# Output product of a hybrid layer: plain products for each tile, against seven half-size products for each pair of tiles with two of the operand sums on GpSimd

## The chip, the core and the metric

The kernel runs on one core of one Trainium2 chip. The time is that of the device in microseconds (us), from one launch; less is better. Everything is computed in float32.

## The reference

A model layer is applied to a prompt of 4096 rows of 1024 values and to a sample stream of 64 rows with an earlier state. The rows are normalised and modulated (h), multiplied with `w_in` (1024 x 3328) and split into a retention part (four heads with a state of 128 x 128 each) and a windowed attention part (eight query heads, two key heads, a sink in each softmax). Both give 512 columns a row, and these are multiplied with `w_out`:

```python
r_out = _head_norm(r_out).reshape(B, L, RET_WIDTH).astype(x.dtype) * jax.nn.silu(rg)
...
a_out = a_out * jax.nn.silu(ag)
y = jnp.concatenate([r_out, a_out], axis=-1) @ w_out
x = x + gate * y
...
y_prompt = _rmsnorm(xp, final_g)
```

The product with `w_out` (1024 x 1024) over all rows is what the change rewrites.

## The kernel before

The rows are cut into 33 tiles of 128: 32 of the prompt (`NT`), and one (`SAMPLE`) whose lower half is the sample. TensorE gets float32 accuracy from three passes: each operand is split into a rounded high part and the remainder (`hh`/`hl`, `wh`/`wl`), and `dense` adds high x high, high x low and low x high in one PSUM bank. A product of a tile with 512 columns of weights is thus 3 x 8 matmuls of 128x512; two such products make a tile's output, 48 matmuls.

There are two phases, each a loop over the tiles (`phase_tiles`), and each engine has its own program; semaphores order them. Phase A (`slot`) makes the four 512-column groups of the retention half, the retention itself, and writes each tile's h and its gated retention rows `yr` to DRAM scratch. Phase B (`slot_b`) loads h again, makes keys and values (`dense_kv`, 24 matmuls of 128x256), queries and gates (two products), the scores of the tile before (`scores`), masks them and takes the row maximum (`mask_max` on VectorE), takes the exponentials (`softmax` on ScalarE), turns p by a round trip through DRAM and a block transpose (`turn_p`), weighs the values (`weigh`), and makes the output of the tile two back from `yr` and the attention rows, with its gate, the residual, the final norm and the store.

The order within a tile is that of the code on each engine. All transfers are issued by SyncE's queue (SP) in program order; one that waits holds back all behind it. `store_blocks` and `load_blocks` issue four transfers each.

## Time and profile before

| | |
|---|---|
| median of 3 runs | 1877.16 us (1875.1 to 1878.53) |
| the profiled execution | 1879.75 us, span of its core 1878.0 us |
| TensorE busy | 1811.4 us, 96% of the span |
| VectorE busy | 1158.3 us, 62% |
| ScalarE busy | 533.6 us, 28% |
| GpSimd busy | 114.3 us, 6% |
| DMA | 314.23 MB, 60.0% of the 16 engines |
| TensorE in the chain that ended last | 90% of the span |

Busy shares are averages over the phases. The chain of waits follows the last instruction back to what released each step, so it tells which engine the time went through.

### The profile page before, as it was taken

What the parts mean: (1) busy time and instruction counts of PE and PEld (TensorE: products, weight loads), DVE (VectorE), ACT (ScalarE), POOL (GpSimd) and SP (SyncE); (2) the same over time, 40 slices, a digit from 0 to 9 for tenths busy, and PEclk for the clock granted to TensorE, in tenths of its full rate; (3) what the DMA queues carried; (4) which work ended last, traced back from release to release, by engine and by line L of the source; (5) the groups of instructions that cost most, each with busy time, mean ns of one, the idle gap of its engine ahead of it and who ended that gap; (6) DMA issues with size and microseconds to landing.
All of it is one profiled execution on the core that took longest, in us unless ns stands there. A gap on an engine that the chain in (4) does not pass through costs nothing.

```text
span 1878.0 us, 30820 instructions
## 1 busy us (share of the span) xinstructions
PE 1811.4 (96%) x9636; PEld 1499.0 (80%) x9636; DVE 1158.3 (62%) x2742; ACT 533.6 (28%) x1471; POOL 114.3 (6%) x278
## 2 busy tenths in 40 slices
PE   6899999999999999999699999999999999999995
PEld 3678888888888888888578888888888888888884
DVE  3655666556566655667566676666666666666664
ACT  3312212212221221223332333333333333333321
POOL 1000000000000000010000000000000000000000
PEclk8999999999999999999899999999999999999998
DMA  9655555555555555554667567557567567566573
GB/s 373 226 153 141 128 149 144 128 140 139 136 134 148 145 125 144 136 152 131 186 176 211 158 172 210 158 174 206 162 177 198 166 181 192 167 186 190 160 187 102
DMA packets 489513, 314.23 MB, mean 167 GB/s; under 512 B 349554, under 2 KB 424498, under 8 KB 488452
## 3 DMA queue, kind: packets, MB, share of 16 engines
q1 hardware_dynamic: 489476, 313.77, 60.0%
q8 instruction: 19, 0.31, 0.1%
q14 instruction: 18, 0.15, 0.0%
HBM read 183.31 MB, written 130.36 MB: 167 GB/s over the span
## 4 chain that ended last, share of the span: by engine, by line
PE 90%; issue 4%; DMA 3%; DVE 1%; SPq 1%; POOL 0%; ACT 0%; POOLq 0%; DVEq 0%; ACTq 0%
PE bank L1245 78%; PE bank L1439 3%; PE bank L1418 3%; PE bank L1343 1%; PE bank L1335 1%; PE bank L1341 1%; PE bank L1329 1%; DMA xn_scratch<-xn 1%; DMA aqk_row<-aqk_scratch 1%; SPq L402 1%; PE bank L1398 0%; DMA xp<-xn_scratch 0%; SPq L489 0%; DMA out_gate<-gate_scratch 0%; POOL small L621 0%
## 5 line engine op out<-in xcount | busy, mean ns | idle before, releaser
L1245 PE MATMUL bank<-wh,hh 128*128 128x512 f32 x1584 | 400.9, 395 | 15.3 <-DVE k_row L904 6.1
L1245 PE MATMUL bank<-wl,hh 128*128 128x512 f32 x1584 | 393.2, 391 | 0.0
L1245 PE MATMUL bank<-wh,hl 128*128 128x512 f32 x1584 | 393.1, 390 | 0.0
L1245 PEld LDWEIGHTS bank<-wh,hh 128*128 128x128 f32 x1584 | 294.4, 190 | 77.3 <-issue 12.3
L1245 PEld LDWEIGHTS bank<-wl,hh 128*128 128x128 f32 x1584 | 298.6, 189 | 62.3
L1245 PEld LDWEIGHTS bank<-wh,hl 128*128 128x128 f32 x1584 | 298.3, 188 | 62.0
L703 ACT ACTIVATE hf<-xn,tiny_a 128x128 f32<-128x128 f32 (+1 forms) x248 | 98.6, 480 | 374.0 <-DVE xn L879 374.0
L1172 DVE SCALAR_TENSOR_TENSOR a_gate<-a_gate,bank 128x128 f32<-128x128 f32 x132 | 29.1, 283 | 205.8 <-ACT a_gate L836 205.8
L775 ACT ACTIVATE s_row<-p_in,tiny_b 128x256 f32<-128x256 f32 x264 | 130.9, 500 | 49.8 <-DVE tiny_b L1082 49.8
L1245 PE MATMUL bank<-wh,yh 128*128 128x512 f32 x528 | 133.1, 395 | 6.9 <-DVE yl L1113 6.9
L1245 PE MATMUL bank<-wl,yh 128*128 128x512 f32 x528 | 130.4, 389 | 0.0
L1245 PE MATMUL bank<-wh,yl 128*128 128x512 f32 x528 | 130.4, 389 | 0.0
L1245 PEld LDWEIGHTS bank<-wh,yh 128*128 128x128 f32 x528 | 100.8, 191 | 28.3 <-DVE yl L1113 7.1
L1245 PEld LDWEIGHTS bank<-wl,yh 128*128 128x128 f32 x528 | 99.1, 188 | 20.6
L1245 PEld LDWEIGHTS bank<-wh,yl 128*128 128x128 f32 x528 | 99.1, 188 | 20.6
L1007 DVE SCALAR_TENSOR_TENSOR r_gate<-r_gate,bank 128x512 f32<-128x512 f32 x33 | 22.7, 688 | 140.1 <-ACT r_gate L751 140.1
L1076 DVE CUSTOM_DVE_ANT_0 p_in<-bank,mask 128x256 f32<-128x256 f32 x264 | 96.2, 421 | 1.1 <-issue 1.1
L1090 DVE STREAM_TRANSPOSE s_row<-p_in 128x1024 f32<-128x1024 f32 x66 | 81.6, 1237 | 3.4 <-DMA p_in<-p_scratch 3.3
L924 DVE TENSOR_TENSOR s_t<-bank,decay 128x512 f32<-128x512 f32 x33 | 22.8, 692 | 94.9 <-PE bank L1329 94.9
L836 ACT ACTIVATE a_gate<-bank 128x256 f32<-128x256 f32 x66 | 21.7, 381 | 156.8 <-PE bank L1245 156.8
L664 POOL TENSOR_TENSOR v_prev<-v_row,small 128x128 f32<-128x128 f32 x31 | 12.4, 399 | 858.4 <-PE bank L1439 858.4
L879 DVE STREAM_TRANSPOSE xn<-xp 128x1024 f32<-128x1024 f32 x31 | 38.6, 1245 | 41.2 <-DMA xp<-xn_scratch 41.2
(159 smaller groups left out, 2289.9 us busy)
## 6 DMA issues: line engine op xcount, KB each, us to landing
p_scratch<-s_row SPq DMA_DIRECT2D x264, 128.0 KB, 2.2
p_in<-p_scratch SPq DMA_DIRECT2D x66, 512.0 KB, 4.4
xt<-in_x_prompt SPq DMA_DIRECT2D x64, 512.0 KB, 3.8
h_scratch<-hf SPq DMA_DIRECT2D x33, 512.0 KB, 2.9
hf<-h_scratch SPq DMA_DIRECT2D x33, 512.0 KB, 4.7
out<-xt SPq DMA_DIRECT2D x32, 512.0 KB, 4.9
xn_scratch<-xn SPq DMA_DIRECT2D x31, 512.0 KB, 2.9
xp<-xn_scratch SPq DMA_DIRECT2D x124, 128.0 KB, 3.1
```

Of the source, the lines that this page charges most:

```text
L703: last = nc.scalar.activation(hf[:, k, lo:P], src, ACT.Identity, bias=h_shift[:, k, c:c + 1], scale=h_scale[:, k, c:c + 1])
L775: nc.scalar.activation(s_row[:, half].rearrange("p b (j s c) -> p b j s c", j=4, s=2)[:, :, j, :, :], p_in[:, half, j, :].rearrange("p (s ...
L836: last = nc.scalar.activation(blocked(a_gates[u][:, cols]), by_blocks(ag_bank(i, t)[:, cols]), ACT.Tanh, scale=0.5)
L879: V.transpose(xn[:, :], xp[:, :]).then_inc(x_turned, 1)
L924: V.tensor_tensor(s_t[:, :], qs_b[:, :], decay[:, :], ALU.mult).then_inc(st_done, 1)
L1007: V.scalar_tensor_tensor(r_gate[:, :], r_gate[:, :], 1.0, za1[:, :], ALU.add, ALU.mult).then_inc(rg_done, 1)
L1076: last = V.tensor_tensor_reduce(out=p_in[:, half, j, :], in0=src, in1=m, scale=1.0, scalar=MASKED, op0=ALU.add, op1=ALU.max, accum_out=s_m ...
L1090: V.transpose(s_row[:, half].rearrange("p b n -> p (b n)"), p_in[:, half].rearrange("p b n -> p (b n)")).then_inc(pt_done, 1)
L1172: last = V.scalar_tensor_tensor(ag, ag, 1.0, z, ALU.add, ALU.mult)
L1245: ins = mm(out, a[:, k, :], b[:, k, :], start=first and n == part[0] and k == chunks[0], stop=last and n == part[-1] and k == chunks[-1])
L1418: last = mm(s_banks[2 * half + g][:, jl * 2 * P:(jl + 1) * 2 * P], q[rows, 2 * half + jl, :], k[rows, :, :], start=n == 0, stop=n == 2, ti ...
L1439: last = mm(qv_b[cols, half * 2 * P:(half + 1) * 2 * P], v, p_t[:, :, :, g, s, :], start=s == 0, stop=s == 1, tile_position=(0, g * HD))
```

## The change

The output product leaves phase B and becomes a third phase, C, over pairs of tiles (`phase_pairs`, `window`). Of a pair, the two tiles' `yr` halves are a11 and a21, their attention halves a12 and a22. From these, four sums are made (S1 = a21 + a22, S2 = S1 - a11, S3 = a11 - a21, S4 = a12 - S2), each of 128x512, and seven products of 12 matmuls of 128x512 (`product`, in the order 1, 6, 5, 7, 2, 4, 3) with seven blocks of `w_out`, three of which are themselves sums; seven additions combine the products to the pair's four output quarters. The sample's half pair uses four plain products. S1 and S3 of most pairs are made by GpSimd (`raw_pool`), S2 and S4 by VectorE (`raw_sum`). Here GpSimd also adds the residual (`add_x`), ScalarE makes the high parts (`high`) and VectorE the low ones (`low`).

Around it: the weight blocks are made in phase A's tiles 5 to 12 (`load_prep`, `store_prep`, sums and splits on VectorE and ScalarE), written to scratch, and loaded by GpSimd's queue in phase B (six of 1 MB in its tiles 2 to 7, two in the tiles 30 and 31, six behind the last input product). `yr` is turned in phase A, five tiles late, instead of in phase B. Phase B writes its attention rows to scratch. It turns p two tiles back, its scores stay in PSUM (`mask_max` writes in place, `softmax` reads there), and the high part of h is made by VectorE. The four 1 MB pieces of the gate weights are loaded one a tile (tiles 0 to 3) and used in tile 4, and not all in tile 0.

```diff
+                if static(i) and t < 4:
+                    load_piece(sp, FIRST_GATE + t)
...
-                if mid:
-                    for half in range(2):
-                        wait(sp, exp_done, 2 * (t - 1) + half + 1)
-                        store_blocks(p_dram[2 * (t - 1) + half], s_row[:, half], p_stored[half])
-                    p_back(*prev, 0)
+                if back:
+                    p_back(*same, 0)
+                    gate_out(*same)
+                    p_back(*same, 1)
...
-                    p_back(*prev, 1)
-                    wait(sp, gate_scaled, t)
-                    store_blocks(g_dram[t - 1], a_gates[1 - u][:, :].rearrange("p (b n) -> p b n", b=4), g_stored)
+                    p_out(*prev, 0)
...
+                    p_out(*prev, 1)
...
+            def add_x(i, u, n):
+                p = 2 * i + u
+                xq = xqs[u]
+                src, at = ((c22f, D + COLS), (c11f, 0), (u3f, D), (u2f, COLS))[n]
+                wait(pool, gated, 4 * p + n + 1)
+                wait(pool, xq_loaded[u], 32 * i + 32)
+                nc.gpsimd.tensor_tensor(xq[:, at:at + COLS], xq[:, at:at + COLS], src, ALU.add).then_inc(added, 1)
...
+            def raw_pool(i, u, n):
+                p = 2 * i + u
+                held = {7: 3, 5: 5}[n]
+                wait(pool, op_hi[held], p)
+                wait(pool, op_lo[held], p)
+                wait(pool, in_loaded[u], 64 * i + 64)
+                if n == 5:
+                    wait(pool, raw_done[6], p)
+                    nc.gpsimd.tensor_tensor(s1f, operand_in(u, 0), operand_in(u, 4), ALU.add).then_inc(raw_done[5], 1)
+                else:
+                    nc.gpsimd.tensor_tensor(s34f, operand_in(u, 1), operand_in(u, 0), ALU.subtract).then_inc(raw_done[7], 1)
...
-                    nc.scalar.activation(s_row[:, half].rearrange("p b (j s c) -> p b j s c", j=4, s=2)[:, :, j, :, :],
-                                         p_in[:, half, j, :].rearrange("p (s b c) -> p b s c", s=2, b=4), ACT.Exp,
+                    src = s_banks[2 * half + j % 2][:, (j // 2) * 2 * P:(j // 2 + 1) * 2 * P]
...
-                    last = V.tensor_tensor_reduce(out=p_in[:, half, j, :], in0=src, in1=m, scale=1.0, scalar=MASKED,
+                    last = V.tensor_tensor_reduce(out=src, in0=src, in1=m, scale=1.0, scalar=MASKED,
...
+                if not static(i) or t >= 3:
+                    gated_values(*older)
+                    scale_gate(*same)
+                if mid:
+                    turn_qk(*prev)
+                    qk_low(*prev)
+                if back:
+                    turn_p(*same, 0)
+                    turn_p(*same, 1)
...
+            def raw_sum(i, u, n):
...
+                elif n == 6:
+                    wait(dve, raw_done[5], p + 1)
+                    wait(dve, raw_done[3], p)
+                    V.tensor_tensor(s2f, s1f, a11, ALU.subtract).then_inc(raw_done[6], 1)
+                elif n == 3:
+                    wait(dve, raw_done[6], p + 1)
...
+            def low(i, u, n):
+                p = 2 * i + u
+                wait(dve, op_hi[n], p + 1)
+                raw = ops_raw[n] if n in ops_raw else operand_in(u, n)
+                V.tensor_tensor(ops[n][1], rows4(raw), ops[n][0].bitcast(F32), ALU.subtract).then_inc(op_lo[n], 1)
+            def sum_u2(i, u):
+                p = 2 * i + u
+                wait(dve, m1_kept, p + 1)
+                wait(dve, prod[6], p + 1)
+                wait(dve, added, 4 * p)
+                V.tensor_tensor(u2f, m1f, prod_bank[6][:, :], ALU.add).then_inc(summed, 1)
+            def gate_mult(ap, half, count):
+                wait(dve, summed, count)
+                V.tensor_tensor(ap, ap, out_gate[:, half * COLS:(half + 1) * COLS], ALU.mult).then_inc(gated, 1)
+            def out22(i, u):
+                p = 2 * i + u
+                wait(dve, prod[7], p + 1)
+                wait(dve, summed, 7 * p + 1)
+                wait(dve, added, 4 * (p - 1) + 3)
+                V.tensor_tensor(u3f, u2f, prod_bank[7][:, :], ALU.add).then_inc(summed, 1)
+                wait(dve, prod[5], p + 1)
+                wait(dve, summed, 7 * p + 2)
+                V.tensor_tensor(c22f, u3f, prod_bank[5][:, :], ALU.add).then_inc(summed, 1)
+                V.tensor_tensor(u2f, u2f, prod_bank[5][:, :], ALU.add).then_inc(summed, 1)
+                gate_mult(c22f, 1, 7 * p + 3)
+            def out11(i, u):
+                p = 2 * i + u
+                wait(dve, prod[2], p + 1)
+                wait(dve, added, 4 * (p - 1) + 2)
+                V.tensor_tensor(c11f, m1f, prod_bank[2][:, :], ALU.add).then_inc(summed, 1)
...
+            def final(i, u):
+                p = 2 * i + u
+                wait(dve, rms_step, 3 * p + 3)
+                for n in range(1 if static(i) and p == LAST else 2):
+                    x = xqs[u][:, n * D:(n + 1) * D]
+                    V.scalar_tensor_tensor(x, x, out_rstd[:, n:n + 1], fin_g[:, :], ALU.mult, ALU.mult).then_inc(fin_done, 1)
...
+            def window(i, u):
...
+                if not static(i) or p < LAST:
+                    low(i, u, 3)
+                if not static(i) or p <= LAST:
+                    out12(*before)
+                if not static(i) or p + 1 <= LAST:
+                    low(*nxt, 1)
+                if not static(i) or p < LAST:
+                    sum_u2(i, u)
+                if not static(i) or p + 1 < LAST:
+                    raw_sum(*nxt, 6)
+                final(*before)
+                if not static(i) or p + 1 < LAST:
+                    for n in (6, 5):
+                        low(*nxt, n)
+                if not static(i) or p < LAST:
+                    out22(i, u)
+                if not static(i) or p + 1 < LAST:
+                    low(*nxt, 7)
+                    raw_sum(*nxt, 3)
+                if not static(i) or p < LAST:
+                    out11(i, u)
+                if not static(i) or p + 1 <= LAST:
+                    low(*nxt, 2)
+                if not static(i) or p < LAST:
+                    out21(i, u)
+                if not static(i) or p + 1 < LAST:
+                    low(*nxt, 4)
+                if static(i) and p == LAST:
...
+                if front:
+                    dense_kv(i, u)
+                    wait(pe, aq_done, t)
+                    dense(aq_b[:, :], *h_of(i, t), group(0)).then_inc(zb_ready, 1)
                     scores(*prev)
...
+                    wait(pe, ag_done, t)
+                    dense(ag_b[:, :], *h_of(i, t), group(1)).then_inc(zb_ready, 1)
...
+                    weigh(*same)
...
+            def product(i, u, n, weights=None, first=True, last=True):
+                p = 2 * i + u
+                wait(pe, op_hi[n], p + 1)
...
+                elif n_w == 7:
+                    wait(pe, squared, 4 * p)
+                elif n_w == 1:
+                    wait(pe, m1_kept, p)
+                else:
+                    read = {6: 1, 5: 4, 2: 5, 4: 6, 3: 7}[n_w]
+                    wait(pe, summed, 7 * (p - 1) + read)
+                out = prod_bank[5 if static(i) and p == LAST and n_w == 3 else n_w][:, :]
+                b = block_of[n_w]
+                weight = [[w_block(b, low)[:, j, :] for j in range(4)] for low in range(2)]
+                return dense(out, *ops[n], weight, chunks=range(4), first=first, last=last)
...
+                    product(i, u, 1).then_inc(prod[1], 1)
+                    product(i, u, 1, weights=5, last=False)
...
+                    product(i, u, 5).then_inc(prod[5], 1)
+                    product(i, u, 7).then_inc(prod[7], 1)
+                    product(i, u, 2).then_inc(prod[2], 1)
+                    product(i, u, 4).then_inc(prod[4], 1)
+                    product(i, u, 3).then_inc(prod[3], 1)
```

How instructions stand now, at three places. First SP's queue in phase B's loop. Before, behind the stores of p of tile t-1 (`p_scratch` is the DRAM scratch of p, `aqk_scratch` that of queries and keys):

```order
L489 DMA p_scratch<-s_row 32x4x256
L234 ISA
L514 ISA
L514 DMA p_in<-p_scratch 128x1024
L489 ISA
L489 DMA aqk_scratch<-aqk_row 32x4x160
L489 ISA
```

The changed kernel at the head of a tile, from the last transfer of the gate's store on:

```order
L596 DMA g_scratch<-a_gate 32x4x128
L626 ISA
L626 DMA p_in<-p_scratch 128x1024
L283 ISA
L641 ISA
L641 DMA ya_scratch<-ya_f 128x512
L636 DMA a_gate<-g_scratch 128x512
L596 ISA
L596 DMA aqk_scratch<-aqk_row 32x4x160
```

The second half of p (of tile t-2 now) comes back behind the gate's store; all eight stores of p of tile t-1 stand at the end of the tile, behind the queries' and keys' store.

Second, TensorE. Before, the second of the output's two 512-column products in phase B's loop (`yh`, `yl` are its operands), and the first rows of `weigh`:

```order
L1245 MATMUL bank<-wh,yh 128x512 x8
L1245 MATMUL bank<-wl,yh 128x512 x8
L1245 MATMUL bank<-wh,yl 128x512 x8
L234 REGISTER_ALU
L234 ISA
L1439 MATMUL bank<-s_row,v_prev 64x256 x2
L1439 MATMUL bank<-s_row,v_row 64x256 x2
```

The changed kernel, products 1 and 6 of a pair, the first two of its seven, in phase C's loop (`op_a` and `op_s` are the split operands):

```order
L1728 MATMUL bank<-wh,op_a_h 128x512 x4
L1728 MATMUL bank<-wl,op_a_h 128x512 x4
L1728 MATMUL bank<-wh,op_a_l 128x512 x4
L283 ISA
L1728 MATMUL bank<-wh,op_s_h 128x512 x4
L1728 MATMUL bank<-wl,op_s_h 128x512 x4
L1728 MATMUL bank<-wh,op_s_l 128x512 x4
```

Forty-eight matmuls a tile, 96 a pair, have become 84 a pair, and phase B's loop keeps none of them.

Third, VectorE in phase C's loop, from the low part of S4 to the final norm (`u` and `c` are partial outputs, `m_row` the kept product 1, `xq` the residual rows):

```order
L1563 TENSOR_TENSOR op_s_l<-s_raw,op_s_h 128x512
L283 ISA x2
L1607 TENSOR_TENSOR u<-u,bank 128x512
L283 REGISTER_ALU
L1575 TENSOR_TENSOR u<-u,out_gate 128x512
L283 REGISTER_ALU
L1563 TENSOR_TENSOR op_a_l<-in,op_a_h 128x512
L283 REGISTER_ALU
L1570 TENSOR_TENSOR u<-m_row,bank 128x512
L1552 TENSOR_TENSOR s_raw<-s_raw,in 128x512
L283 ISA
L1615 SCALAR_TENSOR_TENSOR xq<-xq,tiny_c,fin_g 128x1024 x2
```

and GpSimd in the same window:

```order
L875 TENSOR_TENSOR xq<-xq,u 128x512
L283 ISA x2
L887 TENSOR_TENSOR s_raw<-in 128x512
L895 TENSOR_TENSOR tiny_c<-tiny_c 128x2
L283 ISA
L897 TENSOR_TENSOR tiny_c<-tiny_c,small 128x2
L283 REGISTER_ALU x2
L900 TENSOR_TENSOR tiny_c<-tiny_c,small 128x2
L889 TENSOR_TENSOR s_raw<-in 128x512
```

None of this stood in the kernel before. GpSimd's row of line 875 waits for VectorE's row of line 1575, VectorE's of line 1570 for GpSimd's of line 875, and VectorE's of line 1552 for GpSimd's of line 887.

## Rows read from the trace of the kernel before

**Rows 1.** Chain of waits, phase A and phase B: start, length, what (us).

```profile
392.10 21.77 PE bank L1245 x96
...
1263.63 24.85 PE bank L1245 x120
```

**Rows 2.** Windows, one tile of phase A and one of phase B.

```profile
415.00:440.35 25.35, 25.35 (x130) 21.60 (x130) 15.61 (x34) 5.42 (x12) 1.95 (x4) 1.00 0.54 140
1263.63:1291.98 28.35, 28.35 (x161) 23.37 (x161) 18.31 (x50) 9.74 (x32) 1.33 (x4) 1.00 0.63 180
```

**Rows 3.** Timeline of TensorE between the phases: start, length, instruction [idle before].

```profile
894.69 1.20 PE L1245 MATMUL bank<-wkvh,hh 128*128 128x256 f32 x8
...
910.47 1.19 PE L1245 MATMUL bank<-wkvh,yh 128*128 128x256 f32 x8 [1.76 <-DVE a_gate L1172]
...
927.73 0.58 PE L1418 MATMUL bank<-ak_h,aq_h 64*128 64x256 f32 x2 [14.15 <-DVE ak_l L1199]
...
946.66 2.08 PE L1245 MATMUL bank<-wkvh,hh 128*128 128x256 f32 x8 [3.92 <-DVE hl L894]
```

**Rows 4.** Timeline of TensorE at the end.

```profile
1837.49 3.56 PE L1245 MATMUL bank<-wh,yh 128*128 128x512 f32 x8 [6.93 <-DVE yl L1113]
```

**Rows 5.** Timeline of TensorE and VectorE in phase A's tiles 1 and 2.

```profile
85.88 3.54 PE L1245 MATMUL bank<-wh,hh 128*128 128x512 f32 x8 [4.10 <-DVE k_row L904]
122.27 2.56 PE L1245 MATMUL bank<-wh,hh 128*128 128x512 f32 x8 [1.95 <-DVE k_row L904]
81.41 1.25 DVE L879 STREAM_TRANSPOSE xn<-xp 128x1024 f32<-128x1024 f32 x1 [8.39 <-DMA xp<-xn_scratch]
```

**Rows 6.** Timeline of SP's issues in a tile of phase B.

```profile
1267.23 4.20 SPq L489 DMA_DIRECT2D p_scratch<-s_row  x8
1271.57 0.37 SPq L514 DMA_DIRECT2D p_in<-p_scratch  x1
...
1275.69 1.81 SPq L489 DMA_DIRECT2D g_scratch<-a_gate  x4
```

**Rows 7.** Tile p_in: from issue to landing of its loads.

```profile
DMA to landing us min/median/max: 3.6/4.4/5.5
```

**Rows 8.** Timeline of VectorE and ScalarE: one half of a tile's softmax, from its mask on.

```profile
1263.15 0.06 DVE L1072 MEMSET small<- 128x1 f32 x1 [0.40 <-PE bank L1418]
...
1264.89 0.51 ACT L775 ACTIVATE s_row<-p_in,tiny_b 128x256 f32<-128x256 f32 x1 [1.47 <-DVE tiny_b L1082]
...
1266.87 0.19 ACT L779 ACTIVATE tiny_b<-tiny_b 128x4 f32<-128x4 f32 x1
```

**Rows 9.** Page, part 5: VectorE's transpose of p.

```profile
L1090 DVE STREAM_TRANSPOSE s_row<-p_in 128x1024 f32<-128x1024 f32 x66 | 81.6, 1237 | 3.4 <-DMA p_in<-p_scratch 3.3
```

**Rows 10.** Timeline of VectorE in phase A: three operations of 128x512.

```profile
415.41 0.69 DVE L902 TENSOR_TENSOR bank<-bank,rope 128x512 f32<-128x512 f32 x1
416.01 0.68 DVE L904 TENSOR_TENSOR q_row<-bank,rope 128x512 f32<-128x512 f32 x1
416.80 0.69 DVE L907 TENSOR_TENSOR q_row<-q_row,bank 128x512 f32<-128x512 f32 x1
```

**Rows 11.** Groups by line: VectorE's final norm.

```profile
L1145 DVE SCALAR_TENSOR_TENSOR xt<-xt,small,fin_g 128x1024 f32<-128x1024 f32 x33 | 42.2, 1279 | 2.0 <-POOL small L658 2.0
```

**Rows 12.** Timeline of GpSimd in phase B.

```profile
1262.10 0.40 POOL L664 TENSOR_TENSOR v_prev<-v_row,small 128x128 f32<-128x128 f32 x1 [26.85 <-PE bank L1439]
1262.46 0.19 POOL L654 TENSOR_TENSOR small<-small 128x1 f32<-128x1 f32 x1
...
1263.00 0.55 POOL L658 TENSOR_TENSOR small<-small 128x1 f32<-128x1 f32 x1
```

**Rows 13.** Timeline of GpSimd and VectorE near the start.

```profile
34.95 1.46 POOL L618 TENSOR_TENSOR small<-small 128x1 f32<-128x1 f32 x1 [27.16 <-ACT xn L682]
36.48 2.49 POOL L621 TENSOR_TENSOR small<-small 128x1 f32<-128x1 f32 x1
...
34.07 4.49 DVE L319 TENSOR_TENSOR wl<-stage,wh 128x2048 fp32r<-128x2048 f32 x2
```

1133 lines of the change are left out of this document (725 added, 408 removed).

## Prediction

> **What bounds the kernel now.** I read the chain of waits first, then the stretches by window, then single engines. In [rows 1] the chain runs through TensorE in equal pieces: 96 matmuls of 128x512 in 21.77 us in phase A, so 0.2268 us each, and 120 in 24.85 us in phase B. The second window of [rows 2] is one tile of phase B: 28.35 us long and TensorE busy for all 28.35, at a granted clock of 1.00 (2.4 GHz), while VectorE works 18.31 us and ScalarE 9.74. TensorE sets the pace, and whatever leaves it counts in full, as long as nothing else takes its place.
>
> A tile of phase B splits so: the 120 matmuls are 96 wide ones (21.77) and keys and values (24.85 - 21.77 = 3.08); the scores and the weighing are the rest, 28.35 - 24.85 = 3.50. The output product is 48 wide matmuls, 10.89 us.
>
> From the first key matmul at 894.69 [rows 3] TensorE has 33 x (3.08 + 10.89 + 3.50) = 576.5 us without the output, and 33 x 10.89 = 359.2 us of output. That would end at 1830.4; the span ends at 1878.0. The 47.6 us between are lost around the phases' ends: [rows 3] shows idle times of 1.76, 14.15 and 3.92 us, and behind each the matmuls are slow (eight of 256 columns take 2.08 us at 946.66 and 1.20 at 894.69). With about 4 us for that slowness (my estimate from these rows) the start of phase B costs 23.7 us. The end has the other 23.9, with the 6.93 us of [rows 4] in it.
>
> **The product itself.** A pair needs 84 wide matmuls, 19.05 us, where it needed 96, 21.77. Sixteen pairs take 304.8 us and the sample's four products of 12 again 10.9: 315.7 instead of 359.2, which saves 43.5 us. With no loss anywhere TensorE would be done at 1786.9. The seven additions, the sums and the splits are new work of the others; that decides the rest.
>
> **Start of phase A.** VectorE waits 8.39 us for a transfer in tile 1, with 4 MB of gate weights just ahead in the queue, and TensorE then 4.10; two pieces of `w_in` do the same in tile 2, 1.95 [rows 5]. With the slow matmuls behind them (3.54 and 2.56 us for eight, 1.81 at full pace) that is 8 us, and the change spreads or moves these loads. Against it stand four chunks of weight preparation, each 1 MB in and 3.5 MB out in two tiles. Since 4 MB in a burst cost about 6 us and 2 MB about 2.7, I take 2 us a chunk, 8 in all: net 0, bounds -8 and +8. VectorE's sums and splits there and the turn of `yr` lie in its idle time: 15.61 of 25.35 us are busy [rows 2]. Without that cover each would cost its 0.7 to 2.3 us a tile.
>
> **Start of phase B.** Keys have a bank of their own now, so the 1.76 us go. The scores of tile 0 stand behind the queries of tile 1, 8.5 us of work, and SP no longer issues weights, gate, norm weights and `yr` around the load of the queries and keys. What remains is the small load of the sinks, for which VectorE now waits ahead of the turn. I take 5 us idle and 1.5 slow: 6.5 in place of 23.7 (bounds 1 and 15).
>
> **Phase B's pace.** TensorE needs 17.47 us a tile. VectorE loses two gate products, two additions, the norm, a turn and three splits (about 6.6 us) and gets a copy of h, 0.7: 18.3 becomes 12.4, which fits. In-place masking is free by [rows 10], where line 902 writes PSUM in 0.69 us and line 904 SBUF in 0.68. The loop that matters is that of p. From the mask's first row to the end of its half's exponentials pass 3.91 us (1263.15 to 1267.06, [rows 8]). Then SP works in order: four stores 2.1 (half of 4.20), the load of queries and keys 0.37, four stores 2.1, the load of h 0.37, the first half of p 0.37, the gate's stores 1.81 [rows 6], about 0.15 between groups: 11.8 us after the mask the second half's load is issued. It lands 4.4 us later [rows 7], its turn takes 1.24 [rows 9], and behind that turn stands the next tile's mask: 17.4 us around, just TensorE's 17.47. DMA traffic a tile falls only from 5.1 to 3.9 MB (estimate from the sizes of the transfers) in 17.5 instead of 28.35 us, so I expect it to land a little later than now: 17.7 us a tile, +0.2 x 31 = 6.5 us. At the 5.5 us seen as longest it would be 18.5, +32; at 3.6 it is 0.
>
> **Start of phase C.** VectorE has some 49 us of work listed for the last tiles and pairs 0 and 1 where TensorE has 40, and 6 MB of late weights come in beside it. Half of the weights can wait, since products 1, 6, 5, 7 use blocks loaded long before. I take 5 us, bounds 2 and 15. The end behind the last matmul (sum, gate, residual, squares, three GpSimd steps, norm, store) I take as 9 us.
>
> **Phase C's pace.** VectorE has 20 operations of 128x512 and two norms a pair. Operations follow each other every 0.60 to 0.61 us, or 0.79 where one waits for the one before [rows 10]; a norm is 1.28 [rows 11]. Sixteen at 0.61, four at 0.79 and 2.56 make 15.5 us. GpSimd's price for 128x512 no row shows. Its 128x128 takes 0.40 and its one column 0.19 [rows 12], so by the slope about 1.03; the bounds are 0.69, VectorE's own, and 1.6, four times 0.40. In the chain between them (gate, `add_x`, `sum_u2`, S1, S2, the squares' three steps of 1.09 [rows 12], norm) the norm can start 0.69 + 0.05 + 1.03 + 1.03 + 1.09 = 3.9 us after the gate starts, while VectorE has 2.44 us of work: 1.45 idle. Without more that is 16.9 us, under 19.05.
>
> But [rows 13] shows the two engines in each other's way. GpSimd's one-column step takes 1.46 us and its power 2.49, where [rows 12] has 0.19 and 0.55, and both end just as one of VectorE's two subtractions of 2.29 us each (34.07 to 38.56) is over. Those read two tiles in SBUF. Thirteen of VectorE's twenty operations in a window and both norms do too, and all six of GpSimd's. If one keeps out the other, `add_x` falls three times between two such operations, once partly covered by one that reads a bank, and S3 once ahead of the norm: about 3.5 x 1.03 = 3.6 us. The window is then 15.5 + 1.45 + 3.6 = 20.5 us, VectorE paces it, and 15 windows cost 22 us more than TensorE's 19.05. I choose this over 19.05, because the trace shows the exclusion in one direction at least. The Trainium skill, page "SBUF — State Buffer", section "Who interferes with whom", says the same of both: a VectorE instruction with two SBUF inputs contends with a GpSimd instruction that reads SBUF, and who starts first keeps the other out to its end. The trace agrees for GpSimd (1.46 us against 0.19); that VectorE is held too, no row shows.
>
> The page "GPSIMD Engine Reference", section "Elementwise — side-by-side cycle accounting", gives 4497 ns for 2048 columns; scaled to 512 that is an estimate of 1.1 to 1.3 us, and the window would be 21 to 22 us by it.
>
> **The sum.** 1786.9 + 0 + 6.5 + 6.5 + 5 + 9 + 22 = 1836 us as a span, against 1878.0. The median of the runs shown is 0.8 below that span, so 1835.
>
> **Rivals.** *No hold:* VectorE is not kept out, and phase C runs at 19.05: 1813. For it speaks that no VectorE row is seen longer; against it [rows 13].
>
> *GpSimd's two sums do not relieve VectorE:* they take two operations, 1.2 us, off it, and hold it as long. A GpSimd operation of 1.2 to 1.3 us, between the slope and its upper bound, makes the window 21.6 to 22: 1852 to 1859. At 1.6 us it is 23.7, +48: 1883, slower.
>
> *Slower through SP's queue:* a wait takes the place of TensorE's work in phase B. The second half of p is behind 13 other issues; what is late is `turn_p`, behind it in VectorE's order the mask, then the scores' banks, then TensorE. The sum has room for 1878 - 1836 = 42 us, 1.4 us in each of 31 tiles. So a round of 19.1 us decides, with landings of 5.8 us or issues of 0.65 where [rows 6] has 0.52. For it: the round is already 17.4, with denser traffic; against it: 5.5 was the longest landing of 66. With six weight loads of 1 MB in tiles 2 to 7 it can hold there for some tiles. At 19.6 us it gives 1894.
>
> *Gains at the seams fail:* preparation and the two starts at their upper bounds, +25: 1860.
>
> **Chances and range.** The window at 19.5 to 21.5 us and the round near 17.7: 0.48, for 1820 to 1852. No hold: 0.20, for 1803 to 1820. A heavier hold, a round of 18 to 19, or the seams: 0.19, for 1852 to 1873. Within 0.2% (about what a measurement of this kernel can tell from no change, 3.8 us): 0.03. Slower, by the queue or the 23.7 us window: 0.10. Faster is 0.87. The range 1806 to 1870 takes in most of the first three.
>
> **What the changed profile would show.** Pairs of 84 matmuls in phase C with TensorE busy under 95%, at a distance of 20.5 us from pair to pair, VectorE over 85% busy in that stretch, and its subtractions or GpSimd's additions with single durations 0.5 to 1 us over their shortest. At 19.05 us and TensorE busy throughout, the hold was wrong. In phase B tiles 17.5 to 17.9 us apart; if more, VectorE waits at `turn_p` for p_in. The first scores come at about 923 us. GpSimd's 128x512 is at 1.0 to 1.3 us. I am wrong if phase B's tiles are over 18.5 us apart, or the windows over 22.

## The result and the profile after

The changed kernel takes 1974.01 us (median of 4 runs, 1967.41 to 1975.05), the kernel before 1876.22 (1875.1 to 1878.53): a ratio of 1.0516, 95% interval 1.0501 to 1.0531. It is 5.2% slower, where 1835 us was forecast and 1870 was the upper end. The profiled execution took 1975.05 us with a span of 1973.2.

The matmuls did become fewer. TensorE is busy 1806.8 us of that span, where it was 1811.4 of 1878.0, and that includes the matmuls at the lower clock behind each wait. What grew is its idle time: 1973.2 - 1806.8 = 166 us instead of 67. The other part of the loss is in the busy time itself. With 43.5 us of matmuls taken out it should be 1767.9, and it is 39 us more. Some 7 of these are TensorE's own tile of phase B, 17.69 us at a granted clock of 1.00 where the prediction has 17.47; most of the rest should be the lower mean clock, 0.972 instead of 0.985; it was not split further. The windows of the changed kernel say where (stretch, its length, busy time and instructions of each engine, granted clock, DMA share, GB/s); [rows 2] are their counterpart.

```profile
core 0: us, PE busy (x) PEld busy (x) DVE busy (x) ACT busy (x) POOL busy (x), PEclk, DMA share, GB/s
300.00:400.00 100.00, 87.93 (x413) 72.92 (x412) 67.06 (x127) 24.41 (x48) 5.86 (x12) 0.93 0.73 200
...
600.00:928.37 328.37, 326.91 (x1662) 278.00 (x1661) 218.45 (x442) 75.20 (x151) 24.79 (x49) 1.00 0.62 156
928.37:995.21 66.84, 49.88 (x284) 41.14 (x282) 28.11 (x95) 13.82 (x57) 5.40 (x10) 0.90 0.55 157
995.21:1098.85 103.64, 94.21 (x561) 76.49 (x561) 67.96 (x208) 32.55 (x133) 4.28 (x7) 0.93 0.83 252
1098.85:1476.99 378.14, 355.17 (x2243) 285.35 (x2241) 262.73 (x821) 127.31 (x517) 11.10 (x21) 1.00 0.72 214
...
1557.95:1614.34 56.39, 35.72 (x185) 28.20 (x185) 31.59 (x92) 17.41 (x61) 3.57 (x7) 0.82 0.97 330
...
1656.00:1950.00 294.00, 269.50 (x1137) 217.90 (x1136) 248.29 (x298) 98.17 (x214) 143.49 (x123) 0.97 0.39 141
```

From 600 us on, phase A runs as before: 326.91 of 328.37 us busy. Ahead of that, while the weights are prepared, TensorE loses an eighth (87.93 of 100, DMA share 0.73). The first keys stand at 928.37, where [rows 3] have 894.69. The start of phase B (928 to 995) loses 17 us, phase B itself 6 to 10% in every stretch, and the passage to phase C is the worst: 35.72 of 56.39 us busy, the 16 DMA engines 97% occupied at 330 GB/s. In phase C TensorE is busy 269.50 of 294 us, and VectorE 248.29.

| stretch of the profiled execution | forecast | measured | difference |
|---|---|---|---|
| first key matmul (all of phase A) | 894.7 | 928.4 | +33.7 |
| start of phase B, loss: 66.8 us to the fourth tile's keys, less 47.1 of work (keys and queries of three tiles 41.9, one and a half times 3.50) | 6.5 | 19.7 | +13.2 |
| 29 tiles of phase B | 17.7 each | 19.4 each (562.7) | +49.4 |
| passage to phase C, loss: 92.2 us from 1557.95 to pair 2's first product, less 60.9 of work | 5 | 31.3 | +26.3 |
| 14 windows of phase C | 20.5 each | 21.65 each (303.1) | +16.1 |
| end behind the last matmul | 9 | 9 | 0 |

The differences add up to 138.7 us; the span is 137.2 over the 1836 of the sum (the rows of the forecast, added up this way, come to 1834.4). Phase C's pace, the forecast's great doubt, is the smaller part. The rest is waiting around transfers.

**Phase A.** The timeline of the changed kernel in one tile that carries weight preparation (start, length, instruction, idle time before it and what ended it):

```profile
252.03 3.48 PE L1728 MATMUL bank<-wh,hh 128*128 128x512 f32 x8 [5.22 <-DVE k_row L1227]
...
247.55 1.25 DVE L1196 STREAM_TRANSPOSE xn<-xp 128x1024 f32<-128x1024 f32 x1 [9.52 <-DMA xp<-xn_scratch]
...
233.41 3.31 SPq L576 DMA_DIRECT2D stage<-in_w_out  x4
236.76 0.59 SPq L483 DMA_DIRECT2D xn_scratch<-xn  x1
...
241.96 2.94 SPq L468 DMA_DIRECT2D xp<-xn_scratch  x4
```

SP's four loads of the transposed `xn` are issued at 241.96, behind six loads of `w_out`, four of which alone need 3.31 us. VectorE has waited 9.52 us when they land, and TensorE then 5.22. It is the pattern of [rows 5], four times over and longer.

The distances between tiles split the 33.7 us. An undisturbed tile of phase A takes 25.35 us. The nine tiles from 178.07 to 441.08 us, with the preparation's transfers in them, are together 34.9 us over that. The next, with two 1 MB pieces of phase B's weights that SP issues at 437.54, is 5.4 over, and 1.8 lie elsewhere. The loads moved out of the first tiles gave back 8.4: TensorE reaches the same place in its fifth tile at 145.52 instead of 161.14, with 7.2 us of the gate's product still to come. That is the saving of 8 us that the prediction had for them.

**Start of phase B.** Timelines of TensorE, VectorE and SP:

```profile
963.57 0.58 PE L1906 MATMUL bank<-ak_h,aq_h 64*128 64x256 f32 x2 [11.86 <-DVE ak_l L1478]
...
959.63 0.17 DVE L1506 TENSOR_SCALAR tiny_b<-tiny_b 128x8 f32<-128x8 f32 x1 [14.63 <-DMA tiny_b<-in_sink]
...
945.93 1.01 SPq L687 DMA_DIRECT2D tiny_b<-in_sink  x2
946.99 0.50 SPq L616 DMA_DIRECT2D aqk_row<-aqk_scratch  x1
...
948.01 11.04 SPq L468 DMA_DIRECT2D u<-yr_scratch  x4
```

The sinks (two loads of 2 KB) are issued at 945.93 and VectorE's instruction on them starts at 959.63, 13.7 us later. The load of queries and keys behind them lands at 960.8, 13.8 us after its issue, where such a load took 3.3 us in undisturbed tiles. SP itself needs 11.04 us to issue the next four loads. The scores of tile 0 start at 963.57, where I had 923.

**Phase B.** One round of p (VectorE's turn, twice, and SP's issues between):

```profile
1185.69 1.25 DVE L1435 STREAM_TRANSPOSE s_row<-p_in 128x1024 f32<-128x1024 f32 x1 [0.79 <-DMA p_in<-p_scratch]
...
1204.08 1.25 DVE L1435 STREAM_TRANSPOSE s_row<-p_in 128x1024 f32<-128x1024 f32 x1 [0.75 <-DMA p_in<-p_scratch]
...
1191.10 1.81 SPq L596 DMA_DIRECT2D p_scratch<-p_in  x4
1193.10 0.37 SPq L616 DMA_DIRECT2D aqk_row<-aqk_scratch  x1
1193.72 1.88 SPq L596 DMA_DIRECT2D p_scratch<-p_in  x4
...
1197.33 2.00 SPq L596 DMA_DIRECT2D g_scratch<-a_gate  x4
1199.43 0.41 SPq L626 DMA_DIRECT2D p_in<-p_scratch  x1
```

From turn to turn 18.4 us. SP follows the order that the prediction listed: p's first half stored (1191.10), queries and keys, p's second half (1193.72), the gate's four stores (2.00 us, [rows 6] has 1.81), and only then, at 1199.43, the second half's load. VectorE's turn of it starts 4.7 us later. The median landing of such loads is 5.3 us now, 4.4 in [rows 7]. Over these 29 tiles TensorE waits 42.0 us for `hh`, which VectorE splits behind that turn.

**The passage to phase C.**

```profile
1576.14 0.58 POOL L844 DMA_DIRECT2D wh<-wst_scratch  x1
...
1585.05 0.42 SPq L616 DMA_DIRECT2D aqk_row<-aqk_scratch  x1
...
1596.70 0.84 DVE L1467 STREAM_TRANSPOSE aqk_f<-aqk_row 128x640 f32<-128x640 f32 x1 [7.14 <-DMA aqk_row<-aqk_scratch]
...
1599.84 0.58 PE L1906 MATMUL bank<-ak_h,aq_h 64*128 64x256 f32 x2 [14.31 <-issue]
```

Three rows: GpSimd issues six loads of 1 MB from 1576.14 on; SP's load of the sample's queries and keys, issued at 1585.05, lands 11.6 us later beside them; TensorE's scores wait 14.31 us.

**A window of phase C.** VectorE, GpSimd and TensorE:

```profile
1781.04 0.68 DVE L1600 TENSOR_TENSOR u<-u,bank 128x512 f32<-128x512 f32 x1
...
1783.59 1.53 DVE L1563 TENSOR_TENSOR op_s_l<-s_raw,op_s_h 128x512 fp32r<-128x512 f32 x1 [0.16 <-ACT op_s_h L1102]
...
1788.37 0.69 DVE L1570 TENSOR_TENSOR u<-m_row,bank 128x512 f32<-128x512 f32 x1 [1.15 <-POOL xq L875]
...
1791.40 3.51 DVE L1615 SCALAR_TENSOR_TENSOR xq<-xq,tiny_c,fin_g 128x1024 f32<-128x1024 f32 x2 [0.94 <-POOL tiny_c L900]
...
1780.60 1.67 POOL L875 TENSOR_TENSOR xq<-xq,c 128x512 f32<-128x512 f32 x1 [1.95 <-DVE c L1575]
...
1786.62 1.71 POOL L875 TENSOR_TENSOR xq<-xq,u 128x512 f32<-128x512 f32 x1 [2.05 <-DVE u L1575]
1788.29 1.27 POOL L887 TENSOR_TENSOR s_raw<-in 128x512 f32<-128x512 f32 x1
...
1789.14 1.20 PE L1728 MATMUL bank<-wh,op_s_h 128*128 128x512 f32 x4 [2.41 <-ACT bank L1117]
```

`add_x` (line 875) takes 1.67 us and S3 (line 887), with no VectorE instruction of two SBUF inputs beside it for most of its length, 1.27. VectorE's instruction that reads a bank takes 0.68 us with `add_x` beside it; the norm, 2 x 1.28 us in [rows 11], takes 3.51, and the split 1.53. Grouped by line over the stretch (busy us, mean ns | idle before):

```profile
L1615 DVE SCALAR_TENSOR_TENSOR xq<-xq,tiny_c,fin_g 128x1024 f32<-128x1024 f32 x28 | 48.0, 1754 | 13.5 <-POOL tiny_c L900 13.5
L1563 DVE TENSOR_TENSOR op_s_l<-s_raw,op_s_h 128x512 fp32r<-128x512 f32 x52 | 45.6, 896 | 2.1 <-ACT op_s_h L1102 2.1
L1555 DVE TENSOR_TENSOR s_raw<-in,s_raw 128x512 f32<-128x512 f32 x7 | 11.3, 1607 | 0.6
L1570 DVE TENSOR_TENSOR u<-m_row,bank 128x512 f32<-128x512 f32 x14 | 9.6, 687 | 16.7 <-POOL xq L875 16.7
```

### The profile page after: what moved, and what is told of

The parts are those of the page before. It is cut to its first block and busy times, and to the rows that moved or that the text cites. A ratio compares the mean times of both kernels' runs of the same rounds, so it can differ in the third digit from the quotient of the medians.

```text
span 1973.2 us, 30847 instructions
## 1 busy us (share of the span) xinstructions
PE 1806.8 (92%) x9444; PEld 1475.4 (75%) x9444; DVE 1327.2 (67%) x2900; ACT 549.1 (28%) x1544; POOL 262.5 (13%) x338
## 2 busy tenths in 40 slices
DMA packets 518285, 378.66 MB, mean 192 GB/s; under 512 B 352434, under 2 KB 427378, under 8 KB 515396
## 5 line engine op out<-in xcount | busy, mean ns | idle before, releaser
L1728 PE MATMUL bank<-wh,hh 128*128 128x512 f32 x1712 | 443.4, 400 | 32.3 <-DVE k_row L1227 21.8
L1029 ACT ACTIVATE p_in<-bank,tiny_b 128x256 f32<-128x256 f32 x264 | 121.5, 472 | 200.7 <-DVE tiny_b L1426 196.9
L1420 DVE CUSTOM_DVE_ANT_0 bank<-bank,mask 128x256 f32<-128x256 f32 x264 | 104.1, 456 | 1.8 <-issue 1.8
L1728 PE MATMUL bank<-wh,op_s_h 128*128 128x512 f32 x256 | 73.8, 411 | 31.0 <-ACT bank L1117 27.2
L862 POOL TENSOR_TENSOR v_old<-v_new,small 128x128 f32<-128x128 f32 x33 | 17.6, 533 | 617.0 <-PE bank L1924 617.0
L1728 PEld LDWEIGHTS bank<-wh,op_s_h 128*128 128x128 f32 x256 | 48.2, 194 | 47.4 <-ACT bank L1117 21.0
L1728 PE MATMUL bank<-wkvh,hh 128*128 128x256 f32 x256 | 40.4, 302 | 42.9 <-DVE hh L1216 42.9
L1117 ACT ACTIVATE bank<-xq 128x512 f32<-128x512 f32 x64 | 38.5, 602 | 143.2 <-POOL xq L875 143.2
L1728 PE MATMUL bank<-wl,op_s_h 128*128 128x512 f32 x256 | 74.2, 415 | 0.0
L1728 PE MATMUL bank<-wh,op_s_l 128*128 128x512 f32 x256 | 71.5, 403 | 0.0
L875 POOL TENSOR_TENSOR xq<-xq,c 128x512 f32<-128x512 f32 x32 | 52.7, 1648 | 125.6 <-DVE c L1575 125.6
```

Source lines behind the costliest of these rows:

```text
L862: nc.gpsimd.tensor_tensor(v_olds[u][:, :], v_news[u][:, :], zero.to_broadcast([P, P]), ALU.add).then_inc(v_shifted, 1)
L875: nc.gpsimd.tensor_tensor(xq[:, at:at + COLS], xq[:, at:at + COLS], src, ALU.add).then_inc(added, 1)
L1029: nc.scalar.activation(p_in[:, half].rearrange("p b (j s c) -> p b j s c", j=4, s=2)[:, :, j, :, :], src.rearrange("p (s b c) -> p b s c", ...
L1117: nc.scalar.activation(junk[:, :], xqs[u][:, at:at + COLS], ACT.Square, scale=D ** -0.5, accum_out=out_ssq[:, col:col + 1]).then_inc(squar ...
L1420: last = V.tensor_tensor_reduce(out=src, in0=src, in1=m, scale=1.0, scalar=MASKED, op0=ALU.add, op1=ALU.max, accum_out=s_max[:, h:h + 1])
L1728: ins = mm(out, a[:, k, :], b[k], start=first and n == part[0] and k == chunks[0], stop=last and n == part[-1] and k == chunks[-1])
```

## The experiments

Eighteen kernels were run, each with the kernel before beside it on the same chip (medians 1875.5 to 1878.3). Ratios are to that kernel, with 95% intervals. The first letter of a label names the phase that it concerns (`s` the passage, `m` several).

### b1_order: the second half of p ahead of the gate's stores

```diff
 p_back(*same, 0)
-gate_out(*same)
 p_back(*same, 1)
+gate_out(*same)
```

> The changed kernel, with one difference in SP's order in phase B's loop: both halves of p are fetched, then the gate is stored (the gate's four stores stood between the halves). Theory 'SP's order': in the changed kernel the second half's load is issued at 1199.43, although its stores, issued until 1195.60 and landing 2.9 us later, are there at about 1198.5; without the gate's stores ahead of it the loop of p is 0.9 us shorter, so phase B's tiles go from 18.9 to 18.0 us apart, 30 tiles give 20 to 30 us, 1945 to 1955 us in all. Rival 'the transfers themselves': p lands late because the 16 DMA engines are busy (share 0.72), the order of issue does not matter: 1970 to 1978, tiles still 18.9 apart.

1956.44 us, 1.0420 [1.0396, 1.0443]: 18 us under the changed kernel. Tiles in the middle of phase B go from 18.9 to 18.05 us. So the gate's stores ahead of p's load cost about 0.9 us a tile, and the round through SP's queue is what paces phase B.

### a1_order: preparation behind the load of q

```diff
 if second == 1:
     store_prep(c, 0)
+if second == 0:                 # from the end of the slot before,
+    load_prep(c)                # now behind this tile's load of q
 ...
+if second == 1:
+    store_prep(c, 1)
```

> The changed kernel, with the six loads of a chunk of weight preparation and the second pair of its stores issued later: behind the load of xn's blocks and of q's in the next tile, no longer ahead of the store of xn. Same bytes. Theory 'SP's order': TensorE's waits of 5.2 us behind k_row come because the six loads occupy SP for 5.8 us (230.94 to 236.72) ahead of the store of xn; phase A then loses 10 us instead of 34, 1950 us. Rival 'bytes': each chunk's 4.5 MB slow everything, wherever they stand: less than 8 us gained, 1966 or more.

1977.47 us, 1.0528 [1.0504, 1.0551], no gain. Between 150 and 450 us the changed kernel's TensorE waits 16.9 us for `k_row` and 1.0 for `k_t`; here it waits 21.5 us for `k_t` and not for `k_row`. The place in SP's queue is not the cause; the next transfer in line is late instead.

### a2_pool: preparation on GpSimd's queue

```diff
-sp.dma_start(...)      # in load_prep and store_prep
+pool.dma_start(...)    # the same transfers, in GpSimd's slots
```

> The changed kernel, with all loads and stores of the weight preparation issued by GpSimd's queue in phase A, in place of SP's; same bytes, same tiles. Moving them within SP's order (a1_order) gave nothing: the wait only went from k_row to the turned k, since the 5 to 7 us of issue came out of SP's tile wherever they stood. Theory 'SP's time': with SP free of them phase A's tiles 5 to 12 lose less than 12 of their 34 us, 1950 to 1956 in all. Rival 'bytes': 4.5 MB a chunk hold the other transfers up in the DMA engines, phase A ends as late as before, 1970 to 1980.

1967.64 us, 1.0480 [1.0460, 1.0501]; first keys at 919.0, 9.4 earlier. Of the 33.7 us, 9 went with SP's own issuing and 24 stay. SP's row in the same tile shows that its own issuing was not the whole of it:

```profile
233.65 9.30 SPq L468 DMA_DIRECT2D xp<-xn_scratch  x4
```

With no weight traffic in its queue, SP needs 9.30 us to issue these four loads, where the changed kernel's row at 241.96 has 2.94. The DMA engines are 97% busy from 230 to 245 us, with GpSimd's six loads issued from 232.90 on; it is so again in the tiles of the next two chunks (9.40 and 9.01 us). The likeliest reading is that SP is held back by what the other queue has put on the engines. The Trainium skill, page "DMA: Bandwidth & Descriptors", section "Issuing engines are not separate DMA queues", says that all queues share one pool of 16 engines, and that a second issuing engine saves only issue time; the trace agrees, with 9 us of 34 saved.

### a3_spread: preparation over 16 tiles

```diff
-return divmod(t, 2) if static(i) and 0 <= t < 8 else (None, None)
+return divmod(t, 4) if static(i) and 0 <= t < 16 else (None, None)
```

> The changed kernel, with the weight preparation spread over twice as many tiles of phase A: a chunk's first stores (2 MB) in one tile, the second (1.5 MB) in the next, its loads (1 MB) in a third, so that no tile carries more than 2 MB and the 18 MB lie in tiles 5 to 20 (5 to 12 before); all on SP's queue as in the changed kernel. With GpSimd's queue (a2_pool) phase A had only 9 of its 34 us back, and SP's issue of xn's blocks took 9.3 us there. Theory 'bytes in bursts': the DMA engines are 0.62 busy without preparation, two tiles have room for about 2 MB and get 4.5; spread out, phase A loses less than 12 us, so 1950 to 1954. Rival 'each byte or each issue costs wherever it is': the same four chunks cost the same, 1970 to 1978.

The two pieces of phase B's weights move from tile 13 to tile 21 with it. 1953.32 us, 1.0426 [1.0396, 1.0455]: 21 us less. First keys at 909.2, so with the same 18 MB phase A ends 14.5 us late instead of 33.7.

### b2_sinks: the sinks in one piece

```diff
-for g in range(2):
-    sp.dma_start(neg_sink.rearrange("p (j g) -> p j g", g=2)[:, :, g],
-                 sink[:, 4 * g:4 * g + 4].partition_broadcast(P))
+sp.dma_start(den, sink[:, 0:8].partition_broadcast(P))
```

VectorE puts them into the heads' order when it negates them.

> The changed kernel, with the eight sinks loaded in their own order, 32 bytes for each partition in one transfer (in place of two with 4-byte pieces), and brought to the pairs' order by the VectorE instruction that negates them. Theory: the 4-byte pieces take 13.7 us from issue to landing (945.93 to 959.6) and hold the load of the queries and keys behind them (946.99 to 960.8, where 3.3 is usual), and the first scores wait 11.9 us for both. Then the first scores come 8 to 10 us sooner: 1964 to 1967. Rival: the landing is late for the stores of the last tiles ahead of it, or for the mask: no change, 1972 to 1977.

1964.60 us, 1.0456 [1.0435, 1.0477]. VectorE's instruction on the sinks starts 3.0 us after their issue (13.7 before), and SP issues the four loads behind in 2.80 us (11.04 before). TensorE's idle time before the first scores falls from 11.86 to 3.3 us, and the kernel gains 9.4. The Trainium skill, page "DMA: Bandwidth & Descriptors", section "Rules for kernel authors", says that a last dimension that isn't contiguous becomes one descriptor per element. The trace agrees: two loads of 2 KB in such pieces held what came behind them for over 13 us.

### c1_sums: S1 and S3 on VectorE

```diff
-raw_pool(*nxt, 5)
 rms(*before)
-raw_pool(*nxt, 7)
 ...
-raw_sum(*nxt, 6)
+for n in (5, 7, 6):
+    raw_sum(*nxt, n)
```

> The changed kernel, with S1 and S3 of phase C's windows made by VectorE again, GpSimd keeps the residual additions. Theory 'GpSimd's sums hold VectorE as long as they save': the two cost VectorE 1.2 us more a window, and S1's wait (0.7), the norm's lengthening by S3 (0.95) and 0.6 of the wait ahead of the norm go: windows 20.7 in place of 21.6, 12 us gained, 1960 to 1964. Rival 'VectorE's operations count': windows 22.5, 1985 or more.

1961.98 us, 1.0449 [1.0429, 1.0469], 12 us less. Windows are 20.7 us. VectorE does two more operations and the window is shorter: GpSimd's sums do not relieve it.

### c2_vector: the residual additions on VectorE too

```diff
-for n in range(3):
-    add_x(i, u, n)              # GpSimd
+add_v(i, u, n)                  # VectorE, n = 0 to 2 behind their gates, 3 in the next window
```

with the edit of c1_sums.

> The changed kernel, with S1, S3 and the four residual additions of a window all made by VectorE; GpSimd keeps only the three small steps of the norm's factor. Theory 'holds and hand-overs are the window': VectorE has 26 operations of 128x512 and two norms, all at their shortest: 22 x 0.605 + 4 x 0.79 + 2.56 = 19.0 us, and its one wait left is for the squares: windows 19.1 to 19.8, 25 to 33 us gained, 1941 to 1949. Rival 'VectorE is full': six operations more make 21.6 + 3.6 = 25 us, slower by 40 us or more.

1941.16 us, 1.0332 [1.0310, 1.0353]; windows 19.36 us. Groups by line of VectorE in phase C:

```profile
L1616 DVE SCALAR_TENSOR_TENSOR xq<-xq,tiny_c,fin_g 128x1024 f32<-128x1024 f32 x30 | 37.2, 1281 | 9.6 <-POOL tiny_c L900 9.6
L1554 DVE TENSOR_TENSOR op_s_l<-s_raw,op_s_h 128x512 fp32r<-128x512 f32 x56 | 37.2, 684 | 0.0
L1609 DVE TENSOR_TENSOR xq<-xq,c 128x512 f32<-128x512 f32 x30 | 20.5, 685 | 0.0
L1546 DVE TENSOR_TENSOR s_raw<-in,s_raw 128x512 f32<-128x512 f32 x7 | 4.8, 683 | 0.0
```

Every one is at its own length: the norm 1281 ns instead of 1754, the split 684 instead of 896, and additions of two SBUF tiles 683 instead of 1607. The windows of the same stretch:

```profile
1640.00:1920.00 280.00, 279.37 (x1216) 227.42 (x1216) 267.62 (x403) 104.19 (x228) 28.67 (x43) 1.00 0.44 159
```

TensorE is busy 279.37 of 280 us with VectorE at 267.62, its 20 operations and six more in one window. All of this change's 128x512 sums fit on VectorE when GpSimd leaves it alone.

### c4_idle: GpSimd additions that nothing needs

c2_vector, and in ten windows six GpSimd additions of 128x512 whose result is not used:

```diff
+nc.gpsimd.tensor_tensor(idle_out[...], fin_g[:, 0:COLS], fin_g[:, COLS:D], ALU.add)   # six a window
```

> c2_vector, with six additions of 128x512 added on GpSimd in each of ten windows, which read and write SBUF that nobody else uses; nothing waits for their results, and only the first starts ahead of the norm's factor. Theory 'GpSimd's SBUF work holds VectorE': operations of VectorE that read two SBUF tiles get up to 1 us longer while one runs, as in the changed kernel (some 3.1 us a window there): windows 21.5 to 22.5 in place of 19.4, 1962 to 1972 in all. Rival 'only the hand-overs between the engines cost': the additions are free, windows 19.4, 1939 to 1944.

2004.26 us, 1.0692 [1.0663, 1.0721]: 63 us over c2_vector. The ten windows take 23.8 to 27.2 us. No instruction takes anything from these additions, and still:

```profile
1756.94 1.77 DVE L1626 TENSOR_TENSOR xq<-xq,c 128x512 f32<-128x512 f32 x1
...
1756.58 1.59 POOL L907 TENSOR_TENSOR gap<-fin_g 128x512 f32<-128x512 f32 x1 [4.97 <-DVE c L1583]
...
1773.88 4.54 DVE L1633 SCALAR_TENSOR_TENSOR xq<-xq,tiny_c,fin_g 128x1024 f32<-128x1024 f32 x2 [0.59 <-POOL tiny_c L900]
...
1773.81 3.53 POOL L907 TENSOR_TENSOR gap<-fin_g 128x512 f32<-128x512 f32 x2
```

VectorE's addition takes 1.77 us beside one of GpSimd's, the norm 4.54 beside two. Work that VectorE does not depend on stretches its instructions by being there. GpSimd's own steps for the norm stand among the additions in its order, and a later start of these would be another cause. Ten windows of each kernel, c4_idle first, decide between the two:

```profile
1705.31:1963.53 258.22, 212.97 (x841) 171.34 (x840) 250.26 (x287) 74.93 (x163) 112.72 (x87) 0.89 0.35 124
...
1707.34:1900.96 193.62, 193.26 (x841) 156.90 (x840) 185.78 (x280) 73.67 (x161) 20.25 (x30) 1.00 0.44 158
```

For the same 841 matmuls VectorE is busy 250.26 us instead of 185.78, which is 64.5 of the 64.6 us that the ten windows are longer; it is idle 8.0 us in the one and 7.8 in the other. So the whole loss is longer VectorE instructions, and none of it later hand-overs. I had expected windows of 21.5 to 22.5: the direction was right, the size too small.

The Trainium skill, page "SBUF — State Buffer", section "Who interferes with whom", was right in both directions: a VectorE instruction with two SBUF inputs and a GpSimd one that reads SBUF shut each other out, while one that reads a bank goes undisturbed (0.68 us beside `add_x`).

### c3_bank: product 7 freed from the squares

```diff
-wait(pe, squared, 4 * p)
+wait(pe, summed, 7 * (p - 1) + 2)
```

with ScalarE's squares written to another bank than product 7's.

> The changed kernel, with the squares' throw-away output in PSUM bank 3, which phase C leaves free, from pair 2 on, and not in the bank of product 7; product 7 then waits only for the addition that read its bank. Theory 'VectorE and GpSimd pace the window': TensorE's 27 us of waits ahead of product 7 are only where it meets the pace of the others, windows stay 21.5 us and the time 1970 to 1976. Rival 'the shared bank': the windows fall to about 19.8 us, 20 to 27 us gained, 1947 to 1954.

1972.42 us, 1.0497 [1.0479, 1.0514], no gain. The first four or five windows take 19.0 us, the later ones 21.6 again, and the wait stands at VectorE's splits (12.3 us). The wait of 2.41 us at 1789.14 is a symptom; VectorE and GpSimd set the pace.

### s1_late: four of the six late loads held

```diff
 for n in (2, 4, 3):
+    if n == 4:
+        pool.wait_ge(qk_lo, SAMPLE + 1)
```

> The changed kernel, with four of the six late 1 MB weight loads held by GpSimd until the sample tile's queries and keys are split (two are still issued at once). Theory: TensorE's 14.3 us ahead of the last scores come from the 6 MB in flight, behind which p and the queries and keys land (issued 1585.05, landed 1596.7, 11.6 us where 3.3 is usual); held, they land in 4 to 5 us, TensorE's idle time there falls to 6 us and products 4 and 3 wait a few us for their weights: 8 us gained, 1966. Rival: the weights are then late by as much as was gained, or the wait was VectorE's order: 1972 to 1978.

1972.40 us, 1.0502 [1.0484, 1.0519]. Idle time at the scores falls from 14.3 to 8.7 us and most of it comes back at later waits; the gain of 2 us can't be told from none.

### b3_spread and b4_timed: phase B's weight loads elsewhere

```diff
-early_at = {2 + k: k for k in range(6)}
+early_at = {4 + 3 * k: k for k in range(6)}     # b3_spread
+pool.wait_ge(pt_done, 2 * t - 2)                # b4_timed: behind the turn of p
```

each with the edit of b1_order. In b4_timed each load stays in its tile (2 to 7).

> b1_order, with GpSimd's six 1 MB weight loads of phase B in its tiles 4, 7, 10, 13, 16, 19 (in tiles 2 to 7 before). In b1_order tiles 3 to 7 are 22.0, 27.6, 20.1 us apart where later ones are 18.0. Theory 'the weight loads make it': at one in three tiles each costs under 0.5 us, 10 to 16 us gained over b1_order (1956): 1940 to 1947. Rival 'the cached keys' eight loads and the last tiles of yr, which also stand there on SP, make it': 1953 to 1958.

> b1_order, with GpSimd's six 1 MB weight loads of phase B's tiles 2 to 7 each held until that tile's p is turned, so that they move while the masks and exponentials of the next are made and neither p nor its blocks are on the way. Spreading them over more tiles gave nothing (b3_spread: the tiles that carry one are 3 to 4 us longer, wherever they are). Theory 'a megabyte costs its 3 us only while p is on its way': tiles 3 to 8 come 18 to 19 us apart, 10 to 15 us gained over b1_order (1956): 1941 to 1946. Rival 'bytes cost at any time': 1953 to 1958.

1958.14 us, 1.0434 [1.0404, 1.0463], and 1953.68, 1.0411 [1.0378, 1.0442]. Neither differs from b1_order's 1956.44 by more than the noise. In b3_spread the last five loads stretch their tile and the next by 1.2 to 4.9 us together, 3.6 on the mean, wherever they stand. My expectation fell: not the crowding of the loads costs the time, but the loads themselves.

### b5_none: those six loads left out

The edit of b1_order, and six of the eight early blocks of weights (1 MB each) are not loaded.

```diff
-early_at = {2 + k: k for k in range(6)}
+early_at = {}
```

> b1_order, without the six 1 MB weight loads of phase B's tiles 2 to 7 (products 5, 7 and half of 6's weights are then what the blocks held before; the two loads of tiles 30 and 31 and the six late ones stay). It prices the six loads. Theory: they cost 3 us each, 18 in all: 1936 to 1941, tiles 3 to 8 18 us apart. Rival 'the eight loads of cached keys and the last tiles of yr cost these tiles their time': 1950 or more.

1939.89 us, 1.0336 [1.0304, 1.0369], 16.5 us under b1_order: 2.75 us per MB that travels beside p's round, in that order of SP's queue.

### s2_turn: the queries' load and the sample's turn earlier

```diff
+if front:
+    aqk_in(i, u)
 if mid:
     p_out(*prev, 0)
-if front:
-    aqk_in(i, u)
```

and the sample's queries and keys are turned and split ahead of its gate.

> The changed kernel; SP fetches a tile's queries and keys ahead of the stores of p, and at the start of phase C VectorE and ScalarE turn and split the sample's queries and keys ahead of its gate. The weight loads stay as they are. Theory 'order and bytes share the 14.3 us ahead of the last scores': the load is issued some 9 us sooner, but still behind up to 6 MB; the idle time falls by 4 to 9 us, and phase B's loop of p is 0.4 us a tile shorter: 1952 to 1962. Rival 'bytes alone': the seam stays, 1962 to 1974 from the loop alone.

1955.26 us, 1.0416 [1.0383, 1.0449]. The passage did not change: the wait there is now 17.6 us for ScalarE's exponentials. The 19 us came in phase B, from the other half of the edit: 29 tiles in 541.3 us instead of 562.7, 18.7 each, 17.9 in its undisturbed stretch.

### m1_all, m2_all, m3_all, m4_all: the mends together

m1_all has the edits of a3_spread, b2_sinks, b3_spread, the moved load of s2_turn, s1_late and c2_vector. m2_all adds a2_pool's and s2_turn's in full and has b4_timed's loads in place of b3_spread's. m3_all replaces the six loads by 24 pieces of 256 KB in tiles 2 to 25, has GpSimd load the cached keys in tile 25, and holds four of the late loads until tile 31's p is turned:

```diff
+if static(i) and 2 <= t < 26:
+    pool.wait_ge(pt_done, 2 * t - 2)
+    pool.dma_start(w_block(b, low)[:, j, :], wst_dram[...][:, j, :])
 ...
-pool.wait_ge(qk_lo, SAMPLE + 1)
+pool.wait_ge(pt_done, 2 * SAMPLE)
```

m4_all is m3_all with m1_all's passage.

> All mended: preparation spread (a3_spread), sinks in one piece (b2_sinks), both halves of p ahead of the gate's store (b1_order), weight loads spread over phase B (b3_spread), the queries and keys fetched ahead of the stores of p, four late weight loads held (s1_late), all sums and residual additions on VectorE (c2_vector). If the losses are separate, as the theory has it: 1974 - 19 (b1_order) - 9.5 (b2_sinks) - 33 (c2_vector) - 20 to 24 (a3_spread) - 10 to 16 (b3_spread) - 4 (s1_late) = 1868 to 1878, the kernel before or just under it. Rival 'they overlap, one mended makes another bite': 1890 or more.

> m1_all (1901), with three things more: the preparation's transfers on GpSimd's queue besides being spread, phase B's weight loads held as in b4_timed in tiles 2 to 7, and the sample's queries and keys turned first (s2_turn). Theory of separate losses: 1901 - 5 - 12 - 7 = 1877, the time of the kernel before; 1868 to 1885. Rival: 1890 or more.

> m2_all (1905), with phase B's six weight loads cut into 24 of 256 KB, one in each of the tiles 2 to 25 (behind the turn of p); the eight loads of cached keys issued by GpSimd in tile 25 in place of SP in tile 3; and the four late weight loads held until both halves of tile 31's p are turned (in m2_all they started at 1552.0, and p, fetched at 1556.6, landed at 1570.1). Theory 'only what a round trip has to spare is free, and a quarter of a megabyte is 0.7 us': phase B's tiles 17.7 to 18.1 us apart from tile 2 on, 12 us gained there, and 10 to 14 us at the start of phase C: 1876 to 1884, level with the kernel before or a little over. Rival 'the bytes cost the same in pieces': 1890 or more.

> m3_all, with the start of phase C as in m1_all (the sample's queries and keys turned behind its gate, the four loads held until they are split). Theory: phase B gains as in m3_all; the start of phase C takes what it took in m1_all, from the last keys to the end 377 us: 1880 to 1890. It is slower than m3_all by 2 to 8 us if the round trip of tile 31's p is what the late loads must not meet, and level with it or faster if the later arrival of the weights costs m3_all as much.

| | us | ratio | what is seen |
|---|---|---|---|
| m1_all | 1901.01 | 1.0131 [1.0110, 1.0153] | passage 38.5 us |
| m2_all | 1905.20 | 1.0145 [1.0107, 1.0183] | last tile's keys 9.1 us earlier than m1's, passage 49.8 |
| m3_all | 1900.82 | 1.0128 [1.0109, 1.0146] | tiles 17.7 without a piece, 19.5 with one; passage 44.7 |
| m4_all | 1902.23 | 1.0146 [1.0121, 1.0171] | passage 37.9, given back in the first window; level with m3_all |

The passage here runs from the first product of pair 0 to that of pair 1; in the changed kernel it is 46.3 us. Together the mends take 73 us off, and the best is still 1.3% slower than before. All four expectations fell: separate losses would have given 1868 to 1890, and the four times, 1901 to 1905, are on the side of the rivals.

The profiled executions, cut at the same places as in the table of forecast and measurement, show where:

| us | first keys | start of B | 29 tiles of B | to pair 2 | 14 windows |
|---|---|---|---|---|---|
| changed kernel | 928.4 | 66.8 | 562.7 | 92.2 | 303.1 |
| m1_all | 907.1 | 55.4 | 561.7 | 86.0 | 270.7 |
| m2_all | 904.0 | 58.2 | 553.0 | 99.0 | 270.7 |
| m3_all | 903.3 | 52.6 | 564.0 | 87.5 | 272.3 |
| m4_all | 897.8 | 54.5 | 565.7 | 87.8 | 268.2 |

In phase B the mends cancel each other. b1_order alone brings its 29 tiles to 543.6 us and s2_turn alone to 541.3, but with both orders together they take 553.0 to 565.7, about as long as in the changed kernel. An undisturbed tile falls to 17.69 us, TensorE's own, and a tile with a load gets longer: the last five loads of m1_all stretch their tile and the next by 5.4 us on the mean, where b3_spread has 3.6. So the 73 us lie in the other phases. Why the two orders together bear a load worse was not tried. m2_all is ahead of m1_all by 9 us when the passage begins and loses it there, for its late loads are issued at 1552.0 and the last tile's p, issued at 1556.6, lands at 1570.1 beside them.

A piece costs 1.8 us, 7.2 per MB, more than a whole load of 1 MB does in m1_all (5.4), which has the same order of SP's queue, or in b5_none's order (2.75). SP's rows in m3_all, in a tile with a piece, and in s2_turn:

```profile
1187.96 1.86 SPq L567 DMA_DIRECT2D aqk_scratch<-aqk_row  x4
1193.16 0.37 SPq L587 DMA_DIRECT2D aqk_row<-aqk_scratch  x1
1193.81 1.35 SPq L567 DMA_DIRECT2D p_scratch<-p_in  x3
```

```profile
1183.19 1.88 SPq L596 DMA_DIRECT2D aqk_scratch<-aqk_row  x4
1186.99 0.37 SPq L616 DMA_DIRECT2D aqk_row<-aqk_scratch  x1
1189.62 3.93 SPq L596 DMA_DIRECT2D p_scratch<-p_in  x8
```

In s2_turn, the second of the two, the load of queries and keys goes out at 1186.99, 3.8 us after the store of their rows began, in m3_all it goes out at 1193.16, 5.2 us after it, with the piece issued at 1188.43 beside that store. The fetch is 1.4 us later for it. Whether that delay is what reaches TensorE, and whether another moment for the piece would cost less, was not tried.

## Why the prediction was wrong

It ended on the other side, by five steps. In four of them a transfer, or a chain of small ones, is priced too low or not at all; in the fifth the hold between VectorE and GpSimd is right in kind and too small.

**Start of phase A, "net 0, bounds -8 and +8": the largest wrong price of a transfer.** I priced a chunk of 1 MB in and 3.5 MB out at 2 us, beside a burst of 4 MB that cost 6 us in [rows 5]: 0.44 us per MB where the row gives 1.5. The four cost 34.9 us, so 8.7 each, 1.9 per MB. The saving of 8 set against them came as forecast (8.4); the two pieces of phase B's weights, which no term has, cost 5.4. Of the net 33.7 a2_pool takes 9 off, a3_spread 19; with both the first keys are still 9.3, 8.6 and 3.1 us late (m2_all, m3_all, m4_all, whose phase A is the same), around the bound of 8.

**Start of phase B, "6.5 (bounds 1 and 15)".** I named the sinks' load as what remains and gave it 5 us of idle time; it took 13.7 us to land. b2_sinks shows that its 4-byte pieces were the reason for most of it: without them the kernel gains 9.4 us.

**Phase B's pace, "17.7 us a tile, +0.2 x 31".** The mechanism was right, down to the order of SP's issues: the round of p is the pace, and b1_order and s2_turn, which shorten it, are the two edits that moved the tiles. The sizes were off where traffic enters. The round shown above is 18.4 us; the tiles are 19.4 apart on the mean, 18.9 in the undisturbed middle and 20.7 in tiles 3 to 8, with the weight loads. I had given landings "a little later than now"; they are 5.3 us instead of 4.4, SP's stores 2.00 instead of 1.81. The six weight loads, which the sum left out altogether and only a rival mentioned, cost 16.5 us (b5_none). The page counts 378.66 MB, 64 more than before. The sum priced the preparation's 18, at under a third of the row's price, named the late 6 in its term for phase C's start, and put the rest at nothing.

**The rival "slower through SP's queue" is what happened in phase B** (it shared its chance of 0.10 with a window of 23.7 us); its point of decision, a round of 19.1 us, was passed by the mean tile. My argument against it, "5.5 was the longest landing of 66", came from a kernel whose TensorE paced it and whose queues therefore had slack.

**Start of phase C, "5 us, bounds 2 and 15".** It cost 31.3. I had reckoned that half of the late weights can wait; the program doesn't make them wait, and the first MBs already meet the sample's round trip. s1_late and s2_turn, which each cure one wait, moved it to the next: 6 MB at 330 GB/s are some 19 us, my estimate, in which a small transfer takes 11.6 (13.5 in m2_all), and the sample needs two round trips in turn there. In the mends the passage stays at 37.9 to 49.8 us. This is the part least understood.

**Phase C's pace, "20.5 us".** Measured 21.65, with VectorE busy 84% where I said over 85. The hold between the engines, which I chose over 19.05, is real and goes both ways: c2_vector and c4_idle show it by its removal and by its addition alone. (That no VectorE row had been seen longer, the argument for the rival without a hold, was a gap in the rows of the kernel before.) The term that was mis-sized is the 1.03 us for GpSimd's 128x512, a slope from two small shapes: it is 1.27, and with 1.27 in its place the same sum gives 15.5 + 1.9 + 4.5 = 21.9 us. The Trainium skill, page "GPSIMD Engine Reference", section "Elementwise — side-by-side cycle accounting", gives 4497 ns for 2048 columns; scaled to 512 that was an estimate of 1.1 to 1.3 us, and the trace agrees with its upper end. The rival "GpSimd's two sums do not relieve VectorE" is confirmed by c1_sums.

**The chances.** The three seams had upper bounds of +8, +8.5 and +10, and the rival that added them stood at 1860. They came out at +33.7, +13.2 and +26.3, all beyond their bounds and with phase B's pace beside them. Three of the four have a cause in common: small transfers in a chain, priced from a kernel in which they had slack, now with 64 MB more traffic. (The start of phase B is the exception, where the sinks' own pieces did most of it.) Bounds with a common cause are not missed one at a time, and the range was too narrow for that. Two slips of the working change nothing: the three bounds add up to 26.5 us and not 25, and by its own list the second half of p stands behind 15 issues and not 13.

The saving itself, 43.5 us of TensorE, was real in the places where nothing holds TensorE: its own tile is 17.7 us, and the window 19.36 us in c2_vector. No run had all of it at once. If m3_all's 24 tiles with a piece took s2_turn's 17.9 us instead of 19.5 and nothing else changed, 38 us would go, to about 1862; that is an estimate, and no run reached it.

## What to carry to other kernels

When the engine that sets the pace gets less work, a chain of small transfers that lay just under it becomes the pace, and every further MB in the same stretch then has a price: here 2.75 us for one beside p's round trip, 5.4 in the mended order, 1.5 to 1.9 in phase A's bursts. The price holds for one order of the queue and is not to be carried to another: two reorderings that gained 18 and 19 us each gained nothing in phase B together. So list the traffic that a change adds, stretch by stretch, ahead of its arithmetic, and price it by the worst row of a burst, not by the mean landing of quiet tiles.

Work handed from VectorE to GpSimd is no relief if both read two SBUF tiles, as here: count its time on both.

## What the runs showed of the hardware that I had not expected

- The hold is stronger than one wait per pair: beside two GpSimd additions of 1.77 us each (3.53 the pair) a norm of two instructions took 4.54 us instead of 2.56.
- GpSimd's 128x512 addition takes 1.27 us by itself and 1.67 where a VectorE instruction of two SBUF inputs had started just before it. Ten windows with six additions that nothing needs cost 64.6 us, 64.5 of them VectorE's own busy time.
- With the DMA engines 97% busy, SP's issue of four loads took 9.3 us instead of 2.9 (a2_pool), and the landing of the load of queries and keys (320 KB) went from 3.3 to 11.6 us.
- Two loads of 2 KB in 4-byte pieces took 13.7 us to land, with the DMA engines 28% busy, and in one piece 3.0 us.
- 24 pieces of 256 KB cost 1.8 us each, 7.2 per MB, and loads of 1 MB 5.4 in the same order of SP's queue, 2.75 in b1_order's; whether a piece costs more by number or by moment stays open.
